# A transformer layer on eight cores: the projections' epilogues issued in pairs, and the HGRN blocks' preparation moved between the state steps

## What is computed

```python
u = rms_norm(h, g_pre_mix[l])
proj = u @ w_in[l]
q_d, k_d, v_d, q_h, i_h, f_fw, f_bw, g_h = jnp.split(proj, splits, axis=-1)
...
f = lbb + (1.0 - lbb) * jax.nn.sigmoid(...)
ks = 1.0 - f
logf = jnp.log(f)

def step(S, xs):
    qc, kc, lfc, vc = xs
    cum = jnp.cumsum(lfc, axis=-2)
    inter = jnp.einsum('nbhtk,nbhkv->nbhtv', qc * jnp.exp(cum), S)
    rel = jnp.where(tri, cum[..., :, None, :] - cum[..., None, :, :], -jnp.inf)
    scores = jnp.einsum('nbhtk,nbhsk,nbhtsk->nbhts', qc, kc, jnp.exp(rel))
    intra = jnp.einsum('nbhts,nbhsv->nbhtv', scores, vc)
    last = cum[..., -1:, :]
    S = jnp.exp(last[..., 0, :])[..., None] * S + jnp.einsum('nbhsk,nbhsv->nbhkv', kc * jnp.exp(last - cum), vc)
    return S, inter + intra
```

## Time and profile before

| | us |
|---|---|
| median of 6 runs (lowest, highest) | 9479.56 (9422.01, 9583.85) |
| profiled execution, its own time | 9469.64 |
| its span on core 5, the slowest | 9468.0 |
| spans of the other cores | 9369.4 to 9441.7 |
| TensorE, ScalarE, VectorE busy in the span | 6256.8, 4618.5, 3054.6 |

### The profile page before, as it was taken

The page is one execution under the profiler, slowest core; times in us unless marked ns, Lnnn a source line. Parts: engine busy times, 40 slices in busy tenths (PEclk is TensorE's granted clock), DMA queues, the critical chain, the costliest instruction groups (busy, mean ns, idle before and its releaser), DMA issues.

```text
span 9468.0 us, 140820 instructions; the slowest of 8 cores (9369.4 to 9468.0 us)
## 1 busy us (share of the span) xinstructions
PE 6256.8 (66%) x46858; PEld 4024.5 (43%) x46858; DVE 3054.6 (32%) x6446; ACT 4618.5 (49%) x7531; POOL 3.8 (0%) x26
## 2 busy tenths in 40 slices
PE   0556566667777777777777665554446777877865
PEld 0222222256665566555555433332224544455532
DVE  1444432110000000000000544554225666666644
ACT  1232333267777777777777443333333434344445
POOL 0000000000000000000000000000000000000000
PEclk9777777777788888999999555555658999999987
DMA  5344332120010001000000111113555554555532
GB/s 170 124 135 137 110 115 94 63 59 3 3 25 3 3 3 25 3 3 3 3 3 6 54 54 55 59 58 70 93 90 182 162 158 160 158 163 163 162 120 102
DMA packets 475876, 746.45 MB, mean 79 GB/s; under 512 B 232480, under 2 KB 307360, under 8 KB 467232
## 3 DMA queue, kind: packets, MB, share of 16 engines
q1 hardware_dynamic: 475168, 737.43, 26.5%
HBM read 559.17 MB, written 178.13 MB: 78 GB/s over the span
## 4 chain that ended last, share of the span: by engine, by line
PE 37%; ACT 24%; DVE 18%; issue 12%; DMA 6%; ACTq 1%; DVEq 1%; SPq 1%
PE ps L236 35%; ACT arena L209 22%; DVE arena L221 8%; DVE arena L212 5%; PE ps L239 2%; ACT arena L225 2%; DVE arena L230 2%; DVE arena L216 1%; DMA arena<-w_in 1%; DVE arena L227 1%; DMA arena<-WUPS 1%; DMA arena<-w_up 1%; ACTq L182 1%; DMA arena<-w_down 1%; DVEq L182 1%
## 5 line engine op out<-in xcount | busy, mean ns | idle before, releaser
L236 PE MATMUL ps<-arena 128*128 128x129 bf16 (+5 forms) x44582 | 6020.6, 294 | 1641.4 <-ACT arena L209 800.3
L236 PEld LDWEIGHTS ps<-arena 128*128 128x128 bf16 (+1 forms) x44582 | 3826.8, 111 | 3649.0 <-issue 3007.0
L209 ACT ACTIVATE arena<-ps,arena 128x1024 bf16<-128x1024 f32 (+2 forms) x3004 | 2630.2, 905 | 531.6 <-PE ps L236 511.6
L209 ACT ACTIVATE arena<-arena 128x1 f32<-128x1 f32 (+6 forms) x1873 | 834.8, 455 | 1666.2 <-DVE arena L221 856.7
L239 PE MATMUL ps<-arena 128*128 128x128 bf16 x2276 | 267.2, 290 | 1556.9 <-DVE arena L216 978.5
L221 DVE SCALAR_TENSOR_TENSOR arena<-ps,arena 128x256 f32<-128x256 f32 (+2 forms) x2374 | 1135.3, 495 | 349.1 <-ACT arena L209 210.5
L212 DVE TENSOR_TENSOR arena<-arena 128x256 bf16<-128x256 f32 (+6 forms) x1427 | 792.5, 557 | 1376.1 <-ACT arena L209 1184.7
L209 ACT ACTIVATE arena<-ps 128x512 f32<-128x512 f32 (+3 forms) x943 | 580.1, 636 | 1057.5 <-PE ps L236 1046.6
L230 DVE RECIPROCAL arena<-ps 128x1 f32<-128x1 f32 x264 | 43.9, 166 | 2849.0 <-PE ps L236 2832.8
L239 PEld LDWEIGHTS ps<-arena 128*128 128x128 bf16 x2276 | 204.3, 130 | 1781.1 <-issue 1780.9
L225 ACT ACTIVATE arena<-ps 128x1024 bf16<-128x1024 bf16 (+3 forms) x454 | 347.1, 792 | 908.3 <-PE ps L239 844.2
(11 more groups left out here) (11 smaller groups left out, 170.4 us busy)
## 6 DMA issues: line engine op xcount, KB each, us to landing
arena<-WUPS SPq DMA_DIRECT2D x512, 512.0 KB, 4.4
arena<-x SPq DMA_DIRECT2D x97, 512.0 KB, 4.3
arena<-w_up SPq DMA_DIRECT2D x32, 1024.0 KB, 6.2
H<-arena SPq DMA_DIRECT2D x64, 512.0 KB, 3.6
arena<-H SPq DMA_DIRECT2D x64, 512.0 KB, 4.5
arena<-w_in SPq DMA_DIRECT2D x16, 1024.0 KB, 6.4
LFB<-arena SPq DMA_DIRECT2D x64, 256.0 KB, 2.1
WUPS<-arena SPq DMA_DIRECT2D x32, 512.0 KB, 3.9
```

The costliest lines, as they stand in the source:

```text
L209: self.op("act", lambda e: e.activation(out=out, in_=in_, func=func, **kw), R, W)
L236: self.op("pe", lambda e: e.matmul(out, lhsT=lhsT, rhs=rhs, start=start, stop=stop), R, W, inc=inc)
```

## The change

In `phase_pa` the groups are taken in pairs, (3, 7), (5, 6), (0, 1), (2, 4), and (6, 1), (2, 4) in the blocks of the other half. Both groups' matmuls are called first, then their epilogues step by step in turn. In `phase_hg` `block` is cut into `prep`, `chain` (called once for each of the two state steps) and `finish`; `prep` of block i+1 is called between the two `chain` calls of block i, the loads come two blocks ahead by number, into three buffers in place of two, and the tiles that `prep` hands to `chain` are doubled.

```diff
-                groups = list(range(8)) if own else [1, 2, 4, 6]
+                pairs = [(3, 7), (5, 6), (0, 1), (2, 4)] if own else [(6, 1), (2, 4)]
...
+                for pair in pairs:
+                    sts = []
+                    for g in pair:
+                        pj = bank[cnt["pj"] % 5]
+                        cnt["pj"] += 1
+                        for kc in range(8):
+                            k.mm(pj.ap, u.ap[:, kc, :], win.ap[:, kc, g * 512:(g + 1) * 512], kc == 0, kc == 7,
+                                 [u, win], [pj], inc=(kc == 7))
+                        sts.append(stages_for(g, pj))
+                    for i in range(max(len(x_) for x_ in sts)):
+                        for st in sts:
+                            if i < len(st):
+                                st[i]()
...
-            lf = [k.sb([128, 512], F32, "lf%d" % i) for i in range(2)]
+            lf = [k.sb([128, 512], F32, "lf%d" % i) for i in range(3)]
...
-            def block(spec, s):
+            def prep(spec, i):
...
+            def chain(spec, i, ci):
...
+            def finish(spec, i):
...
             loads(specs[0], 0)
-            for i, sp_ in enumerate(specs):
-                nx = specs[i + 1] if i + 1 < len(specs) else None
-                early = nx is not None and not (nx[0] == 0 and nx[1] == 0)
-                if nx is not None and early:
-                    loads(nx, (i + 1) % 2)
-                block(sp_, i % 2)
-                if nx is not None and not early:
-                    loads(nx, (i + 1) % 2)
+            loads(specs[1], 1)
+            prep(specs[0], 0)
+            for i in range(n):
+                chain(specs[i], i, 0)
+                early = (i + 1 < n) and (i + 1 != i_f0)
+                if early:
+                    prep(specs[i + 1], i + 1)
+                chain(specs[i], i, 1)
+                finish(specs[i], i)
+                if i + 1 < n and not early:
+                    loads(specs[i + 1], (i + 1) % 3)
+                    prep(specs[i + 1], i + 1)
+                if i + 2 < n and (i + 2) != i_f0:
+                    loads(specs[i + 2], (i + 2) % 3)
```

More of the change, by code:

```diff
@@ L632, in phase_hg @@
                 k.memset("pool", Sbf[i].ap, 0.0, [Sbf[i]])
-            lf = [k.sb([128, 512], F32, "lf%d" % i) for i in range(2)]
[L634 to L637, removed]
+            lf = [k.sb([128, 512], F32, "lf%d" % i) for i in range(3)]
+            hq = [k.sb([128, 512], BF16, "hq%d" % i) for i in range(3)]
+            hi = [k.sb([128, 512], BF16, "hi%d" % i) for i in range(3)]
+            hg = [k.sb([128, 512], BF16, "hg%d" % i) for i in range(3)]
+            ob = [k.sb([128, 512], F32, "ob%d" % i) for i in range(3)]
             b_t = k.sb([128, 512], F32, "b_t")
@@ L648, in phase_hg @@
             dec = [k.sb([128, 8], F32, "dec%d" % i) for i in range(2)]
[L649 to L654, removed]
+            qkT2 = [k.sb([128, 8, 128], BF16, "qkT%d" % i) for i in range(2)]
+            qTa2 = [k.sb([128, 4, 128], BF16, "qTa%d" % i) for i in range(2)]
+            qTb2 = [k.sb([128, 4, 128], BF16, "qTb%d" % i) for i in range(2)]
+            for i in range(2):
+                k.memset("dve", qTa2[i].ap, 0.0, [qTa2[i]])
+                k.memset("dve", qTb2[i].ap, 0.0, [qTb2[i]])
+            AT2 = [[k.sb([128, 128], BF16, "AT%d_%d" % (j, i)) for i in range(4)] for j in range(2)]
             osb = [k.sb([128, 512], F32, "osb%d" % i) for i in range(2)]
@@ L710, in block @@
                     k.copy("dve", qTb.ap[:, :, 64:128], qkT.ap[:, 0:4, 64:128], [qkT], [qTb])
[L711 to L714, removed]
                     for hh in range(4):
@@ L717, in block @@
                     for hh in range(4):
-                        a_ = AT[hh]
+                        a_ = AT2[s2][hh]
                         k.tt("dve", a_.ap, bSC[hh].ap, U, ALU.mult, [bSC[hh], cst_t], [a_])
[L720 to L743, removed]
@@ new lines, in chain @@
+            def chain(spec, i, ci):
+                dirn, tb, full = spec
+                s, s2 = i % 3, i % 2
+                Hi_ = hi[s]
+                KHA, KHB, DC = kha[s2], khb[s2], dec[s2]
+                qTa, qTb = qTa2[s2], qTb2[s2]
+                ats = AT2[s2]
+                order = (0, 1) if dirn == 0 else (1, 0)
+                qfirst, qsecond = (qTa, qTb) if dirn == 0 else (qTb, qTa)
+                c = order[ci]
+                sus = []
+                for hh in range(4):
+                    dh = dirn * 4 + hh
+                    hc = slice(hh * 128, (hh + 1) * 128)
+                    if full:
+                        if ci == 0:
+                            k.mm(bOh[hh].ap, qfirst.ap[:, hh, :], Sbf[dh].ap, True, False, [qfirst, Sbf[dh]], [bOh[hh]], inc=False)
+                            k.mm(bOh[hh].ap, ats[hh].ap, Hi_.ap[:, hc], False, True, [ats[hh], Hi_], [bOh[hh]], inc=True)
+                        else:
+                            k.mm(bO2h[hh].ap, qsecond.ap[:, hh, :], Sbf[dh].ap, True, True, [qsecond, Sbf[dh]], [bO2h[hh]], inc=True)
+                    su = bSU[hh]
+                    KHc = KHA if c == 0 else KHB
+                    k.mm(su.ap, KHc.ap[:, hc], Hi_.ap[:, hc], True, True, [KHc, Hi_], [su])
+                    sus.append(su)
+                for hh in range(4):
+                    dh = dirn * 4 + hh
+                    k.stt(S32[dh].ap, S32[dh].ap, DC.ap[:, hh * 2 + c:hh * 2 + c + 1], sus[hh].ap, ALU.mult, ALU.add,
+                          [S32[dh], DC, sus[hh]], [S32[dh]])
+                for hh in range(4):
+                    dh = dirn * 4 + hh
+                    k.copy("act", Sbf[dh].ap, S32[dh].ap, [S32[dh]], [Sbf[dh]])
@@ L744, in block @@
+            def finish(spec, i):
+                dirn, tb, full = spec
+                s, s2 = i % 3, i % 2
+                rows = slice(tb * 128, (tb + 1) * 128)
                 if not full:
                     return
-                o_ = osb[s]
+                o_ = osb[s2]
                 if dirn == 1:
```

67 lines of the change are left out of this document (34 added, 33 removed).

## The result

The changed kernel takes 9660.16 us (median of 8 runs, 9595.30 to 9728.04), the kernel before, run beside it, 9453.53 us (16 runs): a ratio of 1.0218, 95% interval 1.0159 to 1.0276. So it is slower, by some 1.6 to 2.8%, and the median is 15 us from the forecast 9645. The ratios leave out runs in which one die ran at a clearly lower clock than the other; where too few are left for an interval, I compare stages. The profiled execution takes 9606.26 us, its slowest core 4 has a span of 9604.7 us.

What follows compares the result with a forecast made beforehand. No engine is full; the chain of waits round one block bounds each stage. HGRN +225 us and projections -50 us (76 - 114 - 12) add +175 to the profiled 9469.64 us: 9645 us, range 9535 to 9735.

Steps and rivals of the forecast that it cites:

- HGRN: Full blocks wait for loads behind SP's stores: backward 18.4 us for 14.62, forward 22.9 for 18.46; +225 us in sum.
- The first rival: HGRN loads are hidden after all: 15.7 us backward, 17.1 forward, time 9380 us, faster; 8 in 100.
- The other rivals: HGRN's TensorE clock at upper level, 9476 us, 6 in 100; projections' other half gains nothing, 9759 us, 4 in 100.
- State-only blocks: HGRN blocks without a store, where SP runs ahead: 6.15 us for 7.16, -30 us.
- Own blocks: Own-token projections: matmuls of groups 2 and 4 stand alone at the end, +2.3 us a block, 33 blocks, +76 us.
- Other half: Projections of the other half: TensorE's own round remains, 12.6 us for 17.80, 22 blocks, -114 us.
- The sum: Whole kernel: HGRN +225 and projections -50 us give +175 us on 9469.64: 9645 us.

Runs made afterwards that it cites:

- the loads-ahead kernel: The changed kernel with each HGRN block's loads called ahead of the finish of the block before: 9423.37 us (4 runs), beside 9512.81 for the kernel before.

## Why the prediction was right

**HGRN, +225 us forecast, +228 measured.** The forecast was that each full block waits for its load behind a store on SP, and each term of that round held: load to matmul 2.90 forecast, 3.06 and 2.87 measured; to the masks 10.93 and 10.94; updates to the next issue 3.57 and 3.51 backward, 8.13 and 8.07 forward. The experiments show the cause: moving SP's calls, or giving them another queue, removes the loss, each issue put ahead of L adds 0.55 to 0.57 us, and the third buffer does nothing. The Trainium skill's 2.6 us (DMA: Bandwidth & Descriptors, Anatomy of one DMA) was an estimate for another queue; here 2.87 to 3.06 us were measured from issue to matmul, and the trace decides. Issued on GpSimd's queue, the loads of LFB and LFF landed 3.0 and 3.1 us behind their issue (medians).

**The first rival** is what happens once the loads are ahead: 17.21 us forward for my 17.1, and 14.76 backward for 15.7. The copy of bO freed its bank when I allowed (2.28 us behind the updates, for 2.3); what differed is TensorE's clock. I took 10.93 us from the decay matmul to the masks, as at the lower level, but on average it was 10.2. Twelve state-step and twelve decay matmuls in a block of 15.4 us, granted 0.50, and in one of 13.8 us, granted 0.68:

```profile
5680.67:5687.48 6.81, 6.81 (x24) 4.06 (x24) 3.57 (x8) 2.27 (x7) 0.00 (x0) 0.50 0.35 116
5724.11:5729.25 5.14, 5.14 (x24) 3.13 (x24) 2.79 (x7) 2.21 (x7) 0.00 (x0) 0.68 0.49 156
```

So the Trainium skill's double-buffering rule (Trainium Kernel Development and Optimization, Best Practices) holds here when the load is issued a block ahead on its queue; a buffer alone did not do it.

**The other rivals** did not come. In the changed kernel HGRN stayed at a granted clock of 0.50, and the other half of the projections gained even on a core that was granted 0.74 there, as told below.

**State-only blocks** 6.31 for 6.15: the next matmul follows the second updates by 0.25 us, not 0.1.

**Own blocks.** +2.4 us of +2.3 where w_up is converted, but only +0.8 in the 12 blocks after it (+0.5 in the mean of the cores), which I gave the same +2.3: 12 x 1.5 = 18 us too many. The working said that smaller tiles pull it down and then didn't take it.

**Other half.** 10.88 for 12.6, at the end of the range that I put at 11.0; 21 x 1.7 = 36 us. My terms add up to 12.8, not 12.6. The rest is TensorE's clock, 1.00 in place of 0.70: 16 matmuls took 3.62 us for my 4.3, twice a block, and the first of them followed the start of the transposes by 0.44 us for 1.01. In the profile of the loads-ahead kernel a core granted 0.74 took 283.06 / 21 = 13.48. So the projections gave 108 us by the start of attention, not 50.

**The sum.** Stages give 228 - 108 = +120 us for the forecast 175; the mean span of the cores rose by 115. The timed ratio says about +206 (150 to 261). The forecast lies between, and part of its closeness to the median is luck, for two things offset each other: the gain of the projections was put 58 us too small, and the timed runs of the changed kernel had a lower clock than some runs of before, which the forecast doesn't hold (0.775 to 0.800 in the mean of the cores; the profiled one of before had 0.791, others of before up to 0.818). What sets that clock from run to run stays open.

## What to carry to other kernels

On a queue that issues in order, a load's lead is set by what it stands behind: look for the store ahead of it, and ask when that store is released and how soon the load's data are needed. A prefetch by number of blocks and one more buffer changed nothing here while the place in the queue stayed. And after each wait removed, order the work anew: (2, 4) first gained 3.4 to 4.2 us a block while loads bound the block, and lost 1.8 to 2.2 once they didn't. A period cut at a store is only good between blocks that have the store at the same place.

## What the runs showed of the hardware

The same instructions were granted different shares of TensorE's clock from core to core of one execution: with the loads ahead of finish, blocks of the other half took 225.91 / 21 = 10.76 us on core 4, granted 1.00 (2.4 GHz), and 13.48 on core 1, granted 0.74. Attention, 27136 matmuls in each, took about 3210 us at 0.92 to 3375 at 0.79 over the runs. That spread of 165 us in an untouched stage is as large as the effects of this change, so stages were a better measure than times.
